# The softmax band of the hybrid decoder layer selected into 128 columns, and two multiplications given to GpSimd

## The reference

```
s = einsum(q, [previous block of keys, own block]) * 64**-0.5     # 128 queries x 256 keys
dist = q_idx + BLOCK - s_idx
mask = (dist >= 0) & (dist < WINDOW)                               # WINDOW = BLOCK = 128
s = where(mask, s - slopes * dist, -inf)
m = maximum(max(s), sink)
p = exp(s - m) / (sum(exp(s - m)) + exp(sink - m))
o = p @ [values of the previous block, own block] * silu(z)
```

## Time and profile before

| | us |
|---|---|
| median of 3 runs | 1089.53 (1089.48 to 1092.77) |
| profiled execution, its own time | 1090.27 |
| its span in the trace | 1088.5 |
| PE busy | 1064.2 (98%) |
| PEld busy | 846.5 (78%) |
| DVE busy | 688.7 (63%) |
| ACT busy | 532.7 (49%) |
| POOL busy | 115.9 (11%) |

### The profile page before, as it was taken

One profiled execution on the slowest core, in us unless ns is written; L12 is line 12 of the kernel. 1 busy time (PEld: TensorE's weight loads), 2 busy tenths in 40 slices (PEclk: granted clock), 3 DMA queues, 4 the chain that ended last, 5 costly groups with the idle time before them and its releaser, 6 DMA issues.

```text
span 1088.5 us, 19513 instructions
## 1 busy us (share of the span) xinstructions
PE 1064.2 (98%) x7212; PEld 846.5 (78%) x7212; DVE 688.7 (63%) x2081; ACT 532.7 (49%) x1557; POOL 115.9 (11%) x152
## 2 busy tenths in 40 slices
PE   7999999999999999999999999999999999999997
PEld 5877787778778787777887878787787878787885
DVE  5285959584665747576365665757537575758565
ACT  4557675754636454363354535435344555564300
POOL 3413132134100000020000000002000000002210
PEclk9999999999999999999999999999999999999999
DMA  8967475665553626253562551715454343622432
GB/s 282 315 209 262 163 274 195 243 208 183 201 205 109 237 73 235 87 185 98 175 228 93 165 215 46 265 49 185 132 179 157 126 157 128 215 73 63 137 116 77
DMA packets 58430, 183.55 MB, mean 169 GB/s; under 512 B 8480, under 2 KB 21216, under 8 KB 45024
## 3 DMA queue, kind: packets, MB, share of 16 engines
q1 hardware_dynamic: 58192, 182.05, 48.7%
q10 hardware_dynamic: 144, 0.26, 0.1%
HBM read 138.22 MB, written 44.07 MB: 167 GB/s over the span
## 4 chain that ended last, share of the span: by engine, by line
PE 65%; DVE 6%; DMA 2%; issue 1%; ACT 0%; SPq 0%; DVEq 0%
PE bank L849 33%; PE bank L900 10%; PE bank L1137 4%; PE bank L957 2%; PE bank L990 2%; PE bank L972 2%; PE bank L1107 1%; PE bank L1120 1%; PE bank L1117 1%; PE bank L1121 1%; DVE y_cols L1797 1%; DVE y_step L1793 1%; PE bank L1030 1%; PE bank L1045 1%; PE bank L1115 1%
## 5 line engine op out<-in xcount | busy, mean ns | idle before, releaser
L849 PE MATMUL bank<-xr,w 128*128 128x512 f32 x2496 | 653.9, 405 | 7.4 <-DVE xr L1534 7.4
L849 PEld LDWEIGHTS bank<-xr,w 128*128 128x128 f32 x2496 | 449.8, 189 | 101.7 <-issue 9.8
L900 PE MATMUL bank<-wo,y_split 128*128 128x512 f32 x432 | 114.4, 404 | 0.0
L900 PEld LDWEIGHTS bank<-wo,y_split 128*128 128x128 f32 x432 | 77.0, 189 | 14.6 <-issue 0.7
L1582 DVE SCALAR_TENSOR_TENSOR kq<-conv_in,convw_all,kq 128x512 f32<-128x512 f32 x96 | 77.3, 806 | 7.8 <-ACT conv_in L1191 5.8
L1487 ACT ACTIVATE o_scaled<-bank 128x128 f32<-128x128 f32 x64 | 17.7, 277 | 124.5 <-PE bank L1121 124.3
L1353 ACT ACTIVATE score<-score,neg_max 128x256 f32<-128x256 f32 (+1 forms) x128 | 62.7, 493 | 29.0 <-DVE neg_max L1759 29.0
L1919 DVE TENSOR_SCALAR steps<-bank,nb_rk 128x128 f32<-128x128 f32 x64 | 22.3, 348 | 63.9 <-PE bank L1117 63.9
L1922 DVE SCALAR_TENSOR_TENSOR state<-state,cols_all,bank 128x128 f32<-128x128 f32 x64 | 22.2, 347 | 63.2 <-PE bank L1120 63.2
L1793 DVE TENSOR_TENSOR y_step<-blocks,y_cols 128x60 f32<-128x60 f32 (+14 forms) x240 | 50.3, 210 | 12.1 <-DMA blocks<-n_spill 3.3
L783 POOL TENSOR_TENSOR xr<-y_tile,xr 128x256 fp32r<-128x256 f32 x8 | 6.0, 774 | 455.1 <-ACT xr L1172 455.1
(11 more groups left out here) (217 smaller groups left out, 1628.3 us busy)
## 6 DMA issues: line engine op xcount, KB each, us to landing
w<-w_split SPq DMA_DIRECT2D x78, 1024.0 KB, 5.4
w_split<-w SPq DMA_DIRECT2D x26, 1024.0 KB, 5.1
blocks<-n_spill SPq DMA_DIRECT2D x32, 256.0 KB
y_spill<-y_out SPq DMA_DIRECT2D x30, 256.0 KB, 5.8
x_tile<-w_in SPq DMA_DIRECT2D x13, 512.0 KB, 6.1
y_tile<-w_in SPq DMA_DIRECT2D x12, 512.0 KB, 6.4
y_tile<-y_spill SPq DMA_DIRECT2D x12, 512.0 KB, 6.1
x_tile<-x SPq DMA_DIRECT2D x12, 512.0 KB, 3.9
```

Of the source, the lines that this page charges most:

```text
L849: ins = nc.tensor.matmul(bank[JOBS[at].bank][:], w[:, turn % 3, wp, k, :], xr[:, xp, k], start=(step == 0), stop=(step == 3 * KT - 1))
L900: ins = nc.tensor.matmul(bank[JOBS[at].bank][:], y_place(t)[:, yp, k], wo[:, k, wp, half * UNIT:(half + 1) * UNIT], start=(step == 0), sto ...
```

## The change: what it does

The scores of a (cc, hd) are still 128 x 256 in the bank. VectorE now first selects: where the column belongs to the own block's past (`recent`), the value of the own block is written over that of the previous block (`copy_predicated`, in the bank, one instruction for each head, 128 x 2 x 128). From there on the score is 128 columns wide: maxima, exponentials and divisions work on half the width, and the bias from the second unit on too. TensorE turns four pieces for each half of a slot instead of eight (six in the first half of slots 0 to 3), all into bank 2; ScalarE copies them with one instruction. The turned weights still mix both blocks, so GpSimd parts them (`part`): one product with the mask `tri` for the own block and one with `past` for the previous block, four instructions of 128 x 256 for each half of a slot. `values` reads the two parts as before.

`values(n, 1)` moves from ahead of the recurrence to the middle of its first step, and VectorE's `gate_b(n, 1)` from ahead of the first `resid` to behind the first `state`.

GpSimd now also multiplies the queries with their decay rows (`decay_query`, 128 x 512, once a slot). Its program is written out by slot: decay rows, parts and the low parts of weights are put between each other, and gain and shift of the output tiles 8 to 10 stand behind all slots.

```diff
+            def part(n, e):
+                if (n, e) == (0, 0):
+                    pool.wait_ge(part_masks, 1)
+                after(pool, p_copied, n, e + 1)
+                for cc in range(2):
+                    for dst, keep in ((p_own, tri), (p_past, past)):
+                        ins = nc.gpsimd.tensor_tensor(dst[:, cc], p_past[:, cc],
+                                                      keep[:].unsqueeze(1).to_broadcast([P, 2, P]), ALU.mult)
+                    ins.then_inc(p_parted.sem, 1)
+            def decay_query(n):
+                after(pool, eg_ready, n, 1)
+                after(pool, qtok_done, n, 1)
+                after(pool, kk_done, n, 2)
+                own = kq[:, n % 2, 1]
+                nc.gpsimd.tensor_tensor(own, own, eg_row[:].rearrange("p t n -> p (t n)"), ALU.mult).then_inc(q_dec_ready.sem, 1)
+            turns = [turn for turn in range(TILES_W) if w_by_pool(turn)]
+            while turns[0] < 9:
+                w_low(turns.pop(0))
+            for n in range(SLOTS):
+                s, i = divmod(n, AH)
+                decay_query(n)
+                if n < AH - 1:
+                    w_low(turns.pop(0))
+                    part(n, 0)
+                    w_low(turns.pop(0))
+                    part(n, 1)
+                    for turn in turns[0:2]:
+                        w_low(turns.pop(0))
+                elif n == AH - 1:
+                    for ks in ((0, 1), (2, 3)):
+                        for k in ks:
+                            wo_low(k)
+                        part(n, ks[0] // 2)
+                    for k in range(4, KT - 1):
+                        wo_low(k)
+                else:
+                    if n == AH:
+                        wo_low(KT - 1)
+                    if i == AH - 1 and s < SBS - 1:
+                        x_low(s + 1, 2)
+                        x_low(s + 1, 3)
+                    part(n, 0)
+                    part(n, 1)
+            for t in POOL_TILES:
+                scale_tile(t)
...
             def turns(n, e):
-                s, i = divmod(n, AH)
-                if e == 1 and i == AH - 1 and s < SBS - 1:
-                    after(pe, ba_summed, s + 1, 1)
                 for cc in range(2):
                     after(pe, p_scaled, n, 4 * e + 2 * cc + 2)
-                    if cc == 0:
-                        after(pe, p_scaled, n, 4 * e + 4)
                     for hd in range(2):
-                        for kb in range(1 if (s, e, cc) == (0, 0, 0) else 2):
-                            q = 2 * hd + kb
-                            ins = nc.tensor.transpose(bank[2 + cc][:, q * P:(q + 1) * P],
-                                                      score[:, cc, hd, kb * P:(kb + 1) * P], ident[:])
-                    ins.then_inc(p_turn_done.sem, 1)
+                        q = 2 * cc + hd
+                        ins = nc.tensor.transpose(bank[2][:, q * P:(q + 1) * P], p_own[:, cc, hd], ident[:])
+                ins.then_inc(p_turn_done.sem, 1)
...
             def copy_turned(n, e):
...
+                after(act, p_turn_done, n, e + 1)
+                nc.scalar.activation(p_past, bank[2][:].rearrange("p (c h n) -> p c h n", c=2, h=2), ACT.Copy)\
+                    .then_inc(p_copied.sem, 1)
...
+                lead = (s, e) == (0, 0)
+                for hd in range(2):
+                    both = bank[2 + hd][:].rearrange("p (c k n) -> p c k n", c=2, k=2)[:, int(lead):]
+                    nc.vector.copy_predicated(both[:, :, 0], recent[:].unsqueeze(1).to_broadcast([P, 2 - int(lead), P]),
+                                              both[:, :, 1]).then_inc(packed.sem, 1)
+                after(dve, packed, n, 2 * e + 2)
                 for cc in range(2):
-                    keys = n_keys(s, 2 * e + cc)
+                    first = P if lead and cc == 0 else 0
                     for hd in range(2):
-                        nc.vector.tensor_tensor_reduce(out=score[:, cc, hd, 0:keys],
-                                                       in0=bank[2 + hd][:, cc * 256:cc * 256 + keys],
-                                                       in1=bias[:, hd, 2 * P - keys:], scale=BD ** -0.5, scalar=LOWEST,
+                        nc.vector.tensor_tensor_reduce(out=p_own[:, cc, hd],
+                                                       in0=bank[2 + hd][:, cc * 256:cc * 256 + P],
+                                                       in1=bias[:, hd, first:first + P], scale=BD ** -0.5, scalar=LOWEST,
...
-                after(dve, qtok_done, n, 1)
-                nc.vector.tensor_tensor(own, own, eg_row[:].rearrange("p t n -> p (t n)"), ALU.mult).then_inc(q_dec_ready.sem, 1)
```

More of the change, by code:

```diff
@@ L940, in scores @@
                 else:
-                    after(pe, p_turned_ready, n, 2)
+                    after(pe, p_copied, n, 1)
                 for cc in range(2):
@@ L1097, in slot @@
                 ins.then_inc(inv_done.sem, 1)
-                values(n, 1)
                 if n == 0:
@@ L1118, in slot @@
                     fill_to(n, at.chunk(c, 2 / 3))
+                    if c == 0:
+                        values(n, 1)
                     after(pe, v_new_ready, n, c + 1)
@@ L1835, in slot @@
                         .then_inc(n_ready.sem, 1)
-                own = kq[:, n % 2, 1]
                 after(dve, n_ready, n, CH)
```

66 lines of the change are left out of this document (29 added, 37 removed).

## The result

The changed kernel takes 1125.87 us (median of 4 runs, 1125.2 to 1126.51), the kernel before 1090.94 (4 runs beside it, 1089.48 to 1092.77). The ratio is 1.032 (95% interval 1.030 to 1.034): slower, as forecast, but by 35 us and not 18. The time is 4.9 above the upper end of the range. The profiled execution took 1125.2, with a span of 1123.1.

A forecast was written before the change was run, and what follows sets the result against it. TensorE's issue plus its few waits for VectorE was taken to bound the kernel: 1090.3 - 13.2 - 1.0 + 18 + 10 + 5 = 1109.1, median 0.7 below, so 1108; range 1088 to 1121.

The forecast's parts named there:

- The turns' term of -13.2: TensorE: 248 turns become 128, each worth its issue distance of 0.11, so 120 fewer give -13.2.
- The price of a product beside the base inverses: VectorE beside GpSimd: each GpSimd product was taken to cost the base inverses 0.45.
- the seven slots without room: Slots 0 to 3, 7, 11 and 12, where TensorE already waits for VectorE's base inverses before the change.
- The -1.0 for the divisions: TensorE: new turns may start after two divisions of four, so wait less: -1.0, bounds 0 and -6.5.
- Select, maxima, divide: VectorE: selected copy 0.42; two and a wait add about 0.8, narrower maxima save about 0.55, divisions 0.25.
- Queries, weights: 0: GpSimd: multiplying queries counted 0, bounds -1 and +3; later low parts of weights in slots 0 to 3 0, 5 worst.
- Part, first half, +18: GpSimd's four products lengthen VectorE's base inverses and TensorE arrives earlier: +18 over all slots; 0 if hidden.
- the middle ones: Slots 5, 6, 9 and 10: about 1.0 of room before L1067; predicted idle there under 1.5.
- Part, second half, +10: Products beside VectorE's convolutions make TensorE wait for the first resid: +10 over the slots, bounds 0 and 22.
- My remark that the later place of the values is no gain: TensorE, second half: moving the values behind resid's wait only brings TensorE to resid sooner, so gains nothing.
- Tile 8, +5: Slot 15: gain and shift follow the second parting, so store and x load come later; VectorE and TensorE 5 late.

The follow-up runs named there:

- the edit: Changed kernel with only output tile 8's gain and shift moved between the two partings of slot 15: 1117.62 us (ratio 1.025).
- both edits: Changed kernel with tile 8 between slot 15's partings and constant matmuls filling TensorE's waits in slots 0 to 3 and 11: 1114.24 us (1.020).

## Why the direction was right and the size wrong

Two steps of the sum failed. The turns' term of -13.2 counted the issue distance of every turn, though behind many of them another engine already ends the next wait: without the parting the kernel is 1088.9 and not the 1078 that my steps give. And TensorE's clock, which costs 9.1 where its waits are filled, was put at nothing. The price of a product beside the base inverses was right.

*Turns, -13.2.* The term as summed failed. A turn is worth 0.10 where TensorE doesn't wait behind it (0.82 for eight in slots 4, 5, 8 and 9) and nothing in slots 0 to 2, where it does. I took the earlier arrival into account at the base inverses, but at resid only loosely: in slots 0 to 2, 6 and 10 VectorE was at its limit there too (with no parting at all, L1152's counterpart waits 0.45 in each of slots 0 to 2 and 0.9 in 6 and 10). With slot 3's collision this makes the base 11 too low. By my steps the kernel without the parting would be 1090.3 - 13.2 - 1.0 + 2.2 (TensorE's earlier arrival in the seven slots without room, 4 x 0.22 + 3 x 0.44) - 0.7 = 1077.6. It is 1088.9. The -1.0 for the divisions was not tested by itself.

*Select, maxima, divide.* The copy was 0.42 as taken, and no cost of the rest shows. I hadn't seen that with fewer turns TensorE moves wo's third low part onto the chain (3.5 in slot 3).

*Queries, weights: 0.* Right for the queries. Slot 3's third group costs 3.5 without the parting too, so it is no price of the order; the parting moves L1103 there by 1.8, as in slots 0 to 2.

*Part, first half, +18.* Mechanism right, 0.45 a product, shown by halving the products and by the writes. Against the kernel without the parting L1103 stands 1.8 later in its slot in slots 0 to 3, 1.0 in 5, 6, 9 and 10, and 17 later in all; without the arrival my term is 16. Idle at L1103 in the seven tight slots was 1.2 to 4.2 (1 to 2.5 forecast) and 0.9 in the middle ones. Slot 3 (4.2) was out, and slot 0 a little (2.8). The page "SBUF — State Buffer" of the Trainium skill says in "SBUF: two separate sides" that whoever starts first has the shared ports for its whole instruction. My reading of that, a full GpSimd instruction on top of each of VectorE's, would have given 2.8 a slot. The halved products moved L1103 by 0.9, which agrees with 0.45 a product, the smaller figure of the earlier trace rows. A lengthened base inverse takes 0.66 and a product 0.70 to the next, so VectorE may have waited only for what was left of each product; this tells against my reading, and not clearly against the page's rule.

*Part, second half, +10.* L1152 does wait for resid in all slots I named, but the waits were scattered: 0.3 instead of 0.6 in slots 4, 5, 8 and 9, 1.6 in 6 and 10, 0.5 instead of 1.2 in 0 to 2, 0.2 to 0.4 in 12 to 14. The waits alone mislead. In slots 0 to 2 TensorE waits 1.3 when its clock is kept up, so the 0.5 is what its slowness left of that. Slots 4 and 8, where L1103 didn't move, are 0.54 longer than without the parting, near the 0.6. I estimate from the slots' lengths, less L1103's shift and the clock's 0.65, that the second half cost 8. My remark that the later place of the values is no gain was wrong: put back to the old place they cost 43. The later place is what hides the parting.

*Tile 8, +5.* Each stage came as worked out: store to load 2.6 (3 taken), VectorE's wait 5.2 and TensorE's 5.4. Slot 15 gets 5.9 shorter by the edit.

*Missing: TensorE's clock.* The sum has no term for it. Its price is shown by the filled waits: 9.1 in the changed kernel, of which 2.4 is slot 15's and is in tile 8's too.

The 18 that are missing are thus 11 for the base (turns without worth and slot 3), and 6 or 7 for the parting and what follows from it, 37.0 instead of 31. There the clock (3.4 to 6.7 outside slot 15) adds what I had left out, the first half was 1 dearer and the second 2 cheaper than I took it, and tile 8 came out at its 5. This division is an estimate, good to a few microseconds, for the effects lap over one another. What makes the clock fall in one slot of a run and not in another that waits as long stays open.

## What to carry to other kernels

Before you count a matmul taken out of the bounding engine, look at the next wait behind it: if that one is already set by another engine, the matmul is worth nothing, and it is that engine's chain that has to get shorter. An idle engine is not a free one when it reads the same memory beside the chain that has no room: here each of its long instructions lengthened one short one by 0.45. And where a change adds waits on TensorE (here 2.4 to 5.4 at a time), give them a second price in the sum, for the clock that may fall with them (here up to 9.1 for six waits).

## What the runs showed that I had not expected

- GpSimd's writes beside VectorE's two-input instructions on SBUF cost these nothing (0.2 each beside 2.31 of writes), its products 0.45 each.
- Added matmuls make a kernel faster (9.1 of 1125.9) where they keep TensorE from waiting 2.4 to 5.4 at a time. Not every such wait had a fall, and a shorter one could: slot 7 waited 2.2 to 2.4 in three of the kernels, and the clock fell in only one (both edits); in slot 12 it fell at a wait of 1.75 with the waits filled and not at one of 1.84 in the changed kernel.
- 128 more turns cost 3.4 in 1089, a quarter of their issue distance, and 6.1 without slot 3, which they made 2.7 shorter by holding back a group of GpSimd's.
